# The down projections in pair-groups of 1024 columns with seven block products, and a new order in the first gate-up group

## The chip, the cores and the metric

The kernel runs on one core of one Trainium2 chip, in one launch. The metric is the device time of that launch in microseconds (us); lower is better. The time before is 2096.84 us, the median of three runs (2096.63 to 2097.2 us).

## The reference

Two transformer layers follow each other on one sequence of 256 tokens with a model width of 2048, all in float32. The first layer (four kinds of attention) and the mixers of the second one are not touched by the change. What matters here is the end of the second layer:

```python
y = _rms(h, norm_ffn_g[i])
h = h + (jax.nn.silu(y @ w_gate[i]) * (y @ w_up[i])) @ w_down[i]
y = _rms(h, norm_ple_g[i])
h = h + jax.nn.sigmoid(y @ w_ple_gate[i]) * (p[i] @ w_ple_proj[i])
return _rms(h, final_norm_g)
```

`w_gate` and `w_up` are 2048 x 5632, `w_down` is 5632 x 2048, `w_ple_gate` is 2048 x 2048 and `w_ple_proj` is 256 x 2048.

## The kernel before

**Exact products from halves.** TensorE multiplies in its fast float32 form only what fits a shortened mantissa, so every operand is held as a high part and a remainder, and each product is three matmuls (`three`, L563): high times high, high times low, low times high. ScalarE makes the high part of a weight tile (`hi`, L1068), VectorE the remainder (`lo`, L1497, which overwrites the raw tile). The weights come from memory once; SyncE issues their loads in order of use.

**Units and rings.** The work is a list of 370 units, made by `plan` (L77). A unit is one weight tile of 128 x 2048 values (four blocks of 128 x 512) and, in the units of interest, 24 matmuls of 512 columns. The raw and `lo` tiles share a ring of 5 places and the `hi` tiles one of 4. Between the first and the last unit of the gate-up stage, and nowhere else, the rings have 7 and 5 places (`R_FFN`, `H_FFN`, and `extended`, L359). `Places.take` gives a unit the place that was used longest ago, and the load waits until the unit that used it last is done on TensorE (L490).

**Order of the work.** Every engine runs a fixed program, a loop over the units. In round u, VectorE does, in this order (L2070 to L2086): `side(u)`, small jobs tied to that round; the first two of three weight sums of a later unit; `hide`; the splits of later units (`split_at`, L380: of unit u + 2 where that belongs to a pair group, of u + 3 for the others); the third weight sum; `cross`; and at a group's last unit `finals` or `post`. ScalarE's loop is alike (L1425). An engine can't go past a waiting step, so a late step holds all that is behind it.

**Gate-up groups.** The 11 groups ("ff", j), units 218 to 337 with the down groups between them, are of kind "pair": one takes 512 columns of the gate and 512 of the up matrix, in eight units of two rows of blocks each. `pair_unit` (L659) makes eight block products of a unit, or, in the three units of a group in `SUMMED`, seven (21 matmuls in place of 24), by a scheme of the Strassen kind. The price of the eighth product is: three sums of weight blocks on VectorE (`weight_sums`, L1512 to L1523, issued in round u - 3), a second tile of `hi` and `lo`, sums of token blocks (XS, made once by `token_sums`), and per group a combination of the crossed sums: P1 is copied to E by ScalarE (`begin_sums`), then four additions (`cross`, L1539). `finals` adds the two halves of psA to E (L1551 left, L1553 right). TensorE's products P2 and P3 write the left half of psA, P4 and P8 the right half, P1, P6, P5 and P7 the four quarters of psB. The next group's first P2 waits for the left final of the group before, its P4 for the right one (`await_product`, L637).

**Hidden values.** `gate_tanh` and `hide` turn E into 512 hidden columns of THF. They are transposed by TensorE in round first + 6 of the next group (`TURNH`, L423) and split there into YH (ScalarE) and YL (`low`, VectorE, L1569).

**Down groups.** Before, there are 12 groups of kind "N", each with 512 columns: 4 units of 24 matmuls after gate-up group 3 and again after group 7, 3 units at the end. Their result is added to X in one instruction (L2046). The last four are followed by the squares of X for the norm, and by transposes of X with `turn_h` (`TURN3`), which the last matrix needs.

**Into the gate-up stage.** The groups ("out2", f), units 202 to 217, end in X updates (L2039 in `post`), each followed by squares (ScalarE), and X is transposed in rounds 208, 212, 216 and 219 (`TURN2`). In round 218 VectorE works out the norm's scales. The first gate-up group takes its eight pairs in the order (1, 3, 0, 5, 2, 6, 4, 7), so that its units with seven products are 220, 222 and 224.

Of the kernel before, what the change touches and what calls it, by code (L numbers as in the profile page):

```python
# [24 lines left out]
UNIT = 2048  # L25

# [29 lines left out]
class Group:  # L56


    def __init__(self, number, name, kind, W, cols, parts, first, seven=()):
# [3 lines left out]
        self.area = number % 2  # L63
# [10 lines left out]
FIRST_ORDER = (1, 3, 0, 5, 2, 6, 4, 7)  # L74


def plan(A):  # L77
# [37 lines left out]
    def down(js, turn, areas):  # L115
        for f in range(4):
            group(("down", 4 * turn + f), "N", A["w_down_2"][0], 512 * f,
                  [[(4 * j + k, 4 * (j % 4) + k) for k in range(4)] for j in js], area=areas[f])

    for j in range(11):  # L120
        order = range(8) if j else FIRST_ORDER
        group(("ff", j), "pair", (A["w_gate_2"][0], A["w_up_2"][0]), 512 * j, [PAIRS[q] for q in order],
              [i for i, q in enumerate(order) if q in SUMMED])
        if j in (4, 8):
            down(range(j - 4, j), j // 4 - 1, (3, 2, 0, 1))
# [6 lines left out]
    freed, crossed = {True: 0, False: 0}, 0  # L132
    for g in groups:
        if g.kind != "pair":
# [20 lines left out]
def build_hybrid(nc, A, C, out, scratch):  # L155
    with ExitStack() as ctx:
# [72 lines left out]
        with ExitStack() as p3:  # L229
# [13 lines left out]
            BS = sb("BS", [128, 512], F32, p3)  # L243
        with ExitStack() as p4:
            XS = sb("XS", [128, 3, 2, 512], F32R, p4)
# [4 lines left out]
            for i in range(R, R_FFN):  # L250
                with ExitStack() as here:
                    raw.append(sb(f"raw{i}", [128, UNIT], F32, here))
                lo.append(sb(f"lo{i}", [128, UNIT], F32R, p4))
        with ExitStack() as p4:
# [4 lines left out]
        XF, SF = E[:, 0, :], E[:, 1, :]  # L259
        with ExitStack() as p5:  # L260
# [77 lines left out]
        xf_made, xs_summed, xs_high, xs_low, weights_summed = [sem(n) for n in (  # L338
            "xf_made", "xs_summed", "xs_high", "xs_low", "weights_summed")]
        e0_made, crossed_over, left_done, finals_made, hb_made = [sem(n) for n in (  # L340
            "e0_made", "crossed_over", "left_done", "finals_made", "hb_made")]
# [80 lines left out]
        TURN3 = {347 + 3 * f: f for f in range(4)}  # L422
        TURNH = {named[("ff", j + 1)].first + 6: j for j in range(10)}  # L423
        TURNH[named[("down", 8)].first] = 10
        HALF = [0] * 10 + [1]
        CROSS = {max(named[("ff", j)].seven): j for j in range(11)}
        TANH = {named[("ff", j)].last + 1: j for j in range(11)}
        HIDE = {named[("ff", j)].last + (4 if j < 10 else 3): j for j in range(11)}
# [44 lines left out]
        def sync_program(e):  # L473
# [10 lines left out]
            for u, (g, i) in enumerate(units):  # L484
# [6 lines left out]
                if g.kind == "pair":  # L491
                    gate, up = [w.rearrange("(k p) n -> p k n", p=128)[:, k0:k0 + 2, g.cols:g.cols + 512] for w in g.W]
                    first, second = ((1, 1), (0, 3)) if u in g.seven else ((0, 1), (2, 1))
                    e.dma_start(two(raw[slot][:, :], *first), gate).then_inc(raw_landed[slot], 16)
                    e.dma_start(two(raw[slot][:, :], *second), up).then_inc(raw_landed[slot], 16)
# [19 lines left out]
        def gpsimd_program(e):  # L515
# [39 lines left out]
            e.wait_ge(unit_done, done(("down", 7)))  # L555
            e.dma_start(PP[:, :, :], A["p_2"][0, 0].rearrange("(t p) c -> p t c", p=128)).then_inc(p_landed, 16)

            e.wait_ge(unit_done, done(("down", 11)))
# [3 lines left out]
        def tensor_program(e):  # L562
# [14 lines left out]
            def await_operand(g, i):  # L577
# [15 lines left out]
                elif name == "down":  # L593
                    e.wait_ge(flip_low, HIDDEN + 4 * (n // 4) + i + 1)
# [20 lines left out]
            def await_bank(g):  # L615
                name, n = g.name
                if name == "down" and n < 8:
                    j, f = 4 * (n // 4) + 4, n % 4
                    if f == 0:
                        e.wait_ge(crossed_over, j + 1)  # L620
                    elif f == 1:
                        e.wait_ge(flip_low, HIDDEN + j)
                    else:
                        e.wait_ge(finals_made, 2 * j + f - 1)
                elif name == "proj":
# [4 lines left out]
                    else:  # L630
                        e.wait_ge(finals_made, 22 + n - 3)
                elif name == "down" and n < 10:
                    bank_freed(("proj", n - 6))
# [3 lines left out]
            def await_product(g, product):  # L637

                j = g.name[1]
                if j == 0:  # L640
# [5 lines left out]
                elif j in (5, 9):  # L646
                    first = j - 5
                    if product in ("P1", "P5", "P2", "P4"):
                        bank_freed(("down", first + {"P1": 1, "P5": 0, "P2": 2, "P4": 3}[product]))
                elif product == "P1":  # L650
                    e.wait_ge(crossed_over, j)
                    if j > 1:
                        e.wait_ge(flip_low, HIDDEN + j - 1)
                elif product == "P2":
                    e.wait_ge(finals_made, 2 * j - 1)
                elif product == "P4":
                    e.wait_ge(finals_made, 2 * j)

            def pair_unit(u):  # L659
                g, i = units[u]  # L660
                j = g.name[1]
# [5 lines left out]
                def tokens(k, t):  # L667
                    return [(XH[:, k, t], XL[:, k, t])]

                def product(name, terms):  # L670
                    first = u == begun.get(name)
                    if first:
                        await_product(g, name)
                    for n, (a, b) in enumerate(terms):
                        x = three(BANKS[name], a, b, first and n == 0, u == ended[name] and n == len(terms) - 1)
# [14 lines left out]
                if u in g.seven:  # L690
                    n = (0, 2, 4).index(k0 // 2)
# [1490 lines left out]
```

## Time and profile before

| | |
|---|---|
| median of three runs | 2096.84 us |
| the profiled execution | 2096.8 us |
| its span, first to last instruction | 2094.9 us |
| TensorE busy | 2078.9 us (99%) |
| VectorE busy | 1402.4 us (67%) |
| ScalarE busy | 956.5 us (46%) |
| granted TensorE clock, mean | 0.999 of 2.4 GHz |
| memory read | 394.62 MB, 189 GB/s over the span |
| the chain that ended last | PE 91%, DVE 6%, ACT 1%, issue 1%, DMA 1% |

The profiled execution's 2096.8 us are its span of 2094.9 us and 1.9 us around it. In the profile PE is TensorE, PEld its weight loads, DVE VectorE, ACT ScalarE, SP SyncE. A matmul's row says 0.39 us while the next one starts 0.23 us later: they overlap, so starts are compared, not lengths. Idle time in brackets is that of the engine just before the instruction, with who ended it.

### The profile page before, as it was taken

Reading aid. Unit: us, or ns where it says so; the run is one execution under the profiler, and the core shown is the slowest. Engines: PE = TensorE matmul, PEld = TensorE weight load, DVE = VectorE, ACT = ScalarE, POOL = GpSimd, SP = SyncE. Lnnn points to the kernel's source line nnn. Section 1 sums busy time; section 2 is a strip of 40 time slices with the busy share of each in tenths; the row PEclk is TensorE's granted clock in tenths of the full one; section 3 lists DMA queues with packets and bytes.
Section 4 is the critical chain, followed back from the end, with each engine's and each line's share of the span. In section 5 each row is a group of like instructions: output and inputs, shape, how many; then the busy total and the mean of one; then the engine's idle time right before and its main releaser. Section 6 shows DMA issues by size and latency. Waiting matters only on the chain.

```text
span 2094.9 us, 25122 instructions
## 1 busy us (share of the span) xinstructions
PE 2078.9 (99%) x10496; PEld 1768.9 (84%) x10496; DVE 1402.4 (67%) x1427; ACT 956.5 (46%) x914; POOL 21.1 (1%) x40
## 2 busy tenths in 40 slices
PE   9999999999999999999999999999999999999998
PEld 8888888888888888888999988788888888888887
DVE  5576555665544455455789858999658986587565
ACT  5544443544343434444444455555435544355443
POOL 2000000000000000000000000000000000000000
PEclk9999999999999999999999999999999999999999
DMA  8655455454555555575655564556645566455553
GB/s 248 217 177 180 162 168 193 161 181 169 193 189 193 196 187 198 183 253 189 203 185 164 178 220 161 186 200 219 220 152 199 199 217 218 149 205 188 187 202 120
DMA packets 226144, 398.38 MB, mean 190 GB/s; under 512 B 12610, under 2 KB 57914, under 8 KB 225776
## 3 DMA queue, kind: packets, MB, share of 16 engines
q1 hardware_dynamic: 222752, 387.64, 54.7%
q0 software_dynamic: 2528, 8.00, 1.3%
q8 instruction: 84, 1.38, 0.3%
q10 hardware_dynamic: 752, 1.12, 0.1%
q14 instruction: 28, 0.23, 0.0%
HBM read 394.62 MB, written 2.12 MB: 189 GB/s over the span
## 4 chain that ended last, share of the span: by engine, by line
PE 91%; DVE 6%; ACT 1%; issue 1%; DMA 1%; ACTq 0%; SPq 0%; DVEq 0%
PE psA L564 23%; PE psA L566 23%; PE psA L565 23%; PE psA L737 6%; PE psA L741 3%; PE psB L564 3%; PE psB L565 3%; PE psB L566 3%; DVE lo L1497 2%; DVE CA L1765 1%; PE psB L794 1%; ACT hi L1068 0%; DVE raw L1521 0%; ACT hi L1072 0%; DMA X<-in_x_dram 0%
## 5 line engine op out<-in xcount | busy, mean ns | idle before, releaser
L1497 DVE TENSOR_TENSOR lo<-raw,hi 128x2048 fp32r<-128x2048 f32 (+3 forms) x401 | 889.1, 2228 | 400.7 <-ACT hi L1068 394.9
L1068 ACT ACTIVATE hi<-raw 128x2048 fp32r<-128x2048 f32 (+3 forms) x368 | 679.6, 1859 | 485.9 <-PE psA L566 355.2
L564 PE MATMUL psA<-hi,XHL 128*128 128x512 f32 (+1 forms) x1434 | 560.9, 391 | 1.6 <-DVE E L1551 1.6
L566 PE MATMUL psA<-hi,XHL 128*128 128x512 f32 (+1 forms) x1434 | 556.8, 388 | 0.0
L565 PE MATMUL psA<-lo,XHL 128*128 128x512 f32 (+1 forms) x1434 | 556.4, 388 | 0.0
L564 PEld LDWEIGHTS psA<-hi,XHL 128*128 128x128 f32 x1434 | 269.4, 188 | 56.8 <-DVE E L1551 2.0
L566 PEld LDWEIGHTS psA<-hi,XHL 128*128 128x128 f32 x1434 | 269.2, 188 | 55.8
L565 PEld LDWEIGHTS psA<-lo,XHL 128*128 128x128 f32 x1434 | 269.5, 188 | 53.9
L564 PE MATMUL psA<-hi,YH 128*128 128x512 f32 x488 | 190.6, 391 | 0.0
L566 PE MATMUL psA<-hi,YL 128*128 128x512 f32 x488 | 189.9, 389 | 0.0
L565 PE MATMUL psA<-lo,YH 128*128 128x512 f32 x488 | 189.9, 389 | 0.0
L564 PE MATMUL psA<-XHL,hi 128*128 128x256 f32 (+1 forms) x528 | 150.4, 285 | 0.5 <-DVE lo L1601 0.5
L565 PE MATMUL psA<-XHL,hi 128*128 128x256 f32 (+1 forms) x528 | 149.5, 283 | 0.0
L566 PE MATMUL psA<-XHL,lo 128*128 128x256 f32 (+1 forms) x528 | 149.4, 283 | 0.0
L737 PE MATMUL psA<-XHL,hi 128*128 128x512 f32 x576 | 138.6, 393 | 0.0
L737 PEld LDWEIGHTS psA<-XHL,hi 128*128 128x128 f32 x576 | 106.0, 188 | 21.5 <-issue 0.6
L566 PEld LDWEIGHTS psA<-hi,YL 128*128 128x128 f32 x488 | 91.6, 188 | 19.1
L564 PEld LDWEIGHTS psA<-hi,YH 128*128 128x128 f32 x488 | 91.6, 188 | 18.7
L565 PEld LDWEIGHTS psA<-lo,YH 128*128 128x128 f32 x488 | 91.6, 188 | 18.7
L1072 ACT ACTIVATE hi<-raw 128x2048 fp32r<-128x2048 f32 x33 | 63.2, 1916 | 93.8 <-DVE raw L1517 83.7
L564 PEld LDWEIGHTS psA<-XHL,hi 128*128 128x128 f32 (+1 forms) x528 | 100.8, 191 | 1.0 <-DVE XHL L1608 0.8
L565 PEld LDWEIGHTS psA<-XHL,hi 128*128 128x128 f32 (+1 forms) x528 | 100.8, 191 | 0.2
(385 smaller groups left out, 2030.0 us busy)
## 6 DMA issues: line engine op xcount, KB each, us to landing
raw<-in_w_in_dram SPq DMA_DIRECT2D x158, 1024.0 KB, 4.9
raw<-in_w_gate_dram SPq DMA_DIRECT2D x88, 512.0 KB, 3.8
raw<-in_w_up_dram SPq DMA_DIRECT2D x88, 512.0 KB, 4.7
raw<-in_w_down_dram SPq DMA_DIRECT2D x44, 1024.0 KB, 5.1
raw<-in_w_out_dram SPq DMA_DIRECT2D x32, 1024.0 KB, 5.1
raw<-in_w_branch_dram SPq DMA_DIRECT2D x16, 1024.0 KB, 5.1
raw<-in_w_ple_gate_dram SPq DMA_DIRECT2D x16, 1024.0 KB, 5.1
raw<-in_w_in_dram SPq DMA_DIRECT2D x16, 512.0 KB, 4.7
```

Of the source, the lines that this page charges most:

```text
L564: e.matmul(dst, A2[0], B2[0], start=first, stop=False, skip_group_check=True)
L565: e.matmul(dst, A2[0], B2[1], start=False, stop=False, skip_group_check=True)
L566: return e.matmul(dst, A2[1], B2[0], start=False, stop=last, skip_group_check=True)
L737: e.matmul(both, hh[:, s], XHL[:, kb, :, :].rearrange("p a t -> p (a t)"), start=i == 0 and n < 2, stop=False, skip_group_check=True)
L741: x = e.matmul(both[:, 256:512], ll[:, s], XH[:, kb, :], start=False, stop=i == len(g.parts) - 1 and n >= 14, skip_group_check=True)
L794: x = e.transpose(ps[:, k, 128 * t:128 * t + 128], src(t, k), ID[:, :])
L1068: e.activation(hi[h_slot[u]][:, m], raw[l_slot[u]][:, m], ACT.Copy).then_inc(hi_made, 1)
L1072: e.activation(hi[th_slot[u]][:, :], raw[t_slot[u]][:, :], ACT.Copy).then_inc(hi_made, 1)
L1497: e.tensor_tensor(lo[l][:, m], raw[l][:, m], hi[h][:, m].bitcast(F32), ALU.subtract).then_inc(lo_made, 1)
L1765: x = e.scalar_tensor_tensor(out=CA[:, c, :], in0=HP[:, c, j:j + 256], scalar=CW[:, 4 * j + c:4 * j + c + 1], in1=CA[:, c, :], op0=ALU.mul ...
```

## The change

The down groups become pair groups of 1024 columns, two for each turn (six in all, with 8, 8, 8, 8, 6 and 6 units; the number of units stays, and the last two groups, 4 and 5, are units 342 to 347 and 348 to 353). The pairs 0 and 2 of each (`HIDDEN_SUMMED`) are made with seven block products. So each has weight sums, a second tile, a `cross` and `finals`, and `add_hidden` adds the crossed sums to X before the finals are added there. The pairs' token sums are now made for the hidden values too (j = 0, 1, 4, 5, 8, 9), in the tiles FORM and FHL, by `copy_block`, `token_sums`, `high_forms` and `low_forms`; the first of the four formed blocks replaces the block of the tokens that isn't used any more. The first gate-up group runs its pairs as (1, 0, 3, 2, 5, 4, 6, 7), with units 219, 221 and 223 as those with seven products, and its first such unit makes its products in another order. `hide` comes a round earlier. The ring sizes and the range in which they are extended stay.

```diff
+USUAL = ("P1", "P6", "P5", "P7", "P2", "P3", "P4")
+LATE = ("P1", "P6", "P2", "P3", "P4", "P5", "P7")
...
-FIRST_ORDER = (1, 3, 0, 5, 2, 6, 4, 7)
+FIRST_ORDER = (1, 0, 3, 2, 5, 4, 6, 7)
+HIDDEN_SUMMED = (0, 2)
+LAST_ORDER = (1, 0, 3, 2, 4, 5)
...
-    def down(js, turn, areas):
-        for f in range(4):
-            group(("down", 4 * turn + f), "N", A["w_down_2"][0], 512 * f,
-                  [[(4 * j + k, 4 * (j % 4) + k) for k in range(4)] for j in js], area=areas[f])
+    w_down = A["w_down_2"][0]
+
+    def down(turn, orders):
+        for q, order in enumerate(orders):
+            group(("down", 2 * turn + q), "pair", (w_down, w_down), (1024 * q, 1024 * q + 512),
+                  [[(16 * turn + 2 * p + k, 2 * p + k) for k in range(2)] for p in order],
+                  [i for i, p in enumerate(order) if p in HIDDEN_SUMMED])
...
-    down((8, 9, 10), 2, (0, 1, 0, 1))
+    down(2, (LAST_ORDER, range(6)))
...
-        TURN3 = {347 + 3 * f: f for f in range(4)}
+        TURN3 = {352: 0, 353: 1, 355: 2, 356: 3}
...
-        HIDE = {named[("ff", j)].last + (4 if j < 10 else 3): j for j in range(11)}
+        HIDE = {named[("ff", j)].last + (2 if j == 10 else 3): j for j in range(11)}
+        SQUARE4 = {352: 0, 353: 1}
...
+                elif name == "ple" and n < 2:
+                    e.wait_ge(finals_made, 2 * named[("down", 5)].pair + n + 1)
...
                     elif product == "P1":
                         e.wait_ge(ss3_made, 4)
+                    elif product == "P5":
                         e.wait_ge(flip_low, SECOND + 4)
...
+            def copy_block(key, turned, half, scale):
+
+                count, slot = FORMS[key]
+                e.wait_ge(flip_turned, turned + 1)
+                if count >= 5:
+                    e.wait_ge(unit_done, named[("down", 2 * ((count - 3) // 2) - 1)].last + 1)
+                e.activation(FORM[slot][:, 0, 0:256], c4(psB[:, half, :])[:, 0, :], ACT.Copy, scale=scale).then_inc(forms_copied, 1)
+
+            def high_forms(key, turned, dst):
+                count, slot = FORMS[key]
+                e.wait_ge(forms_summed, count + 1)
+                e.wait_ge(flip_low, turned + 1)
+                e.activation(dst, FORM[slot][:, 0, 256:384], ACT.Copy).then_inc(forms_high, 1)
+                e.wait_ge(forms_low, 2 * count + 1)
+                e.activation(FHL[slot][:, 0, :], FORM[slot][:, 1, :], ACT.Copy).then_inc(forms_high, 1)
...
+            def token_sums(key, turned, half, scale):
...
+                e.wait_ge(flip_high, turned + 1)
+                e.wait_ge(forms_copied, count + 1)
+                finish(e.scalar_tensor_tensor(out=s1, in0=a22, scalar=scale, in1=a21, op0=ALU.mult, op1=ALU.add))
                 e.tensor_tensor(s3, a11, a21, ALU.subtract)
-                finish(e.tensor_tensor(s1, a21, a22, ALU.add))
                 finish(e.tensor_tensor(s2_, s1, a11, ALU.subtract))
...
+            def low_forms(key, dst, dstH):
+                count, slot = FORMS[key]
+                e.wait_ge(forms_high, 2 * count + 1)
+                e.tensor_tensor(dst, FORM[slot][:, 0, 256:384], dstH.bitcast(F32), ALU.subtract).then_inc(forms_low, 1)
+                e.wait_ge(forms_high, 2 * count + 2)
+                e.tensor_tensor(FHL[slot][:, 1, :], FORM[slot][:, 1, :], FHL[slot][:, 0, :].bitcast(F32),
+                                ALU.subtract).then_inc(forms_low, 1)
...
+            def add_hidden(g):
+
+                c = slice(g.cols[0], g.cols[0] + 1024)
+                e.wait_ge(crossed_over, g.pair + 1)
+                e.tensor_tensor(X[:, 0, c], X[:, 0, c], flat(E[:, 0:2, :]), ALU.add)
+                e.tensor_tensor(X[:, 1, c], X[:, 1, c], flat(E[:, 2:4, :]), ALU.add).then_inc(e_read, 1)
...
+                if u - 1 in TURNH and ("hidden", TURNH[u - 1]) in FORMS:
+                    k = 4 * (TURNH[u - 1] % 4)
+                    low_forms(("hidden", TURNH[u - 1]), YL[:, k, 128:256], YH[:, k, 128:256])
...
+                    if ("hidden", j) in FORMS:
+                        token_sums(("hidden", j), HIDDEN + j, 0, 1.0)
                     low(HIDDEN + j, YL[:, js, :], YH[:, js, :], HALF[j], 1.0)
```

ScalarE calls `copy_block` and `high_forms` in the rounds in which VectorE calls `token_sums` and `low_forms`, ahead of its splits of that round. The places that the rings give by the new plan, where the prediction speaks of them: unit 348 is loaded into the place of unit 344, unit 347 into another one that unit 344 frees, and both loads are issued when unit 344 is done.

## Rows read from the trace of the kernel before

**Rows 1.** The page: busy time of TensorE.
```profile
PE 2078.9 (99%) x10496; PEld 1768.9 (84%) x10496; DVE 1402.4 (67%) x1427; ACT 956.5 (46%) x914; POOL 21.1 (1%) x40
```

**Rows 2.** Waits of TensorE from 1050 us on: us in total, times, longest.
```profile
PE psA L564 <- DVE E L1551: 1.6, 1, 1.6
PE psB L794 <- DVE THF L1560: 1.1, 1, 1.1
PE psB L564 <- DVE XHL L1573: 0.4, 1, 0.4
```

**Rows 3.** Timeline of TensorE: first matmuls of units 258 and 274.
```profile
1486.42 0.39 PE L564 MATMUL psB<-hi,YH 128*128 128x512 f32 x1
...
1573.46 0.39 PE L564 MATMUL psB<-hi,XHL 128*128 128x512 f32 x1
```

**Rows 4.** Timeline of VectorE, gate-up group 1, crossing to left final.
```profile
1342.85 0.69 DVE L1542 TENSOR_TENSOR E<-E,psB 128x512 f32<-128x512 f32 x1 [2.53 <-ACT E L1322]
...
1345.50 1.22 DVE L1521 TENSOR_TENSOR raw<-raw 128x1024 f32<-128x1024 f32 x1
...
1347.36 2.28 DVE L1497 TENSOR_TENSOR lo<-raw,hi 128x2048 fp32r<-128x2048 f32 x1
1349.56 0.69 DVE L1517 TENSOR_TENSOR raw<-raw 128x512 f32<-128x512 f32 x1
1350.16 1.22 DVE L1569 SCALAR_TENSOR_TENSOR YL<-psB,YH 128x1024 fp32r<-128x1024 f32 x1
1351.29 3.95 DVE L1497 TENSOR_TENSOR lo<-raw,hi 128x1536 fp32r<-128x1536 f32 x2
...
1359.83 1.22 DVE L1551 TENSOR_TENSOR E<-E,psA 128x1024 f32<-128x1024 f32 x1
```

**Rows 5.** Timeline of TensorE: the first P2 of gate-up group 2.
```profile
1361.95 0.39 PE L564 MATMUL psA<-hi,XHL 128*128 128x512 f32 x1
```

**Rows 6.** Timeline of ScalarE: the split of unit 235, then of 236.
```profile
1352.64 3.28 ACT L1068 ACTIVATE hi<-raw 128x2048 fp32r<-128x2048 f32 x2
```

**Rows 7.** Timeline of VectorE, rounds 216 to 219.
```profile
1262.04 0.29 DVE L1530 TENSOR_TENSOR E<-E 128x128 f32<-128x128 f32 x1 [5.58 <-ACT E L1081]
1262.24 0.28 DVE L1531 TENSOR_TENSOR E<-E 128x128 f32<-128x128 f32 x1
1262.56 0.29 DVE L1532 TENSOR_TENSOR E<-E 128x128 f32<-128x128 f32 x1
...
1263.50 1.66 DVE L1573 SCALAR_TENSOR_TENSOR XHL<-psB,VC,XHL 128x256 fp32r<-128x256 f32 x4 [0.32 <-ACT XHL L1106]
...
1272.79 1.40 DVE L2039 SCALAR_TENSOR_TENSOR X<-X,SM,psA 128x512 f32<-128x512 f32 x2
1275.73 0.16 DVE L1494 TENSOR_REDUCE SM<-SM 128x2 f32<-128x8 f32 x1 [1.54 <-ACT psB L1114]
...
1278.59 3.96 DVE L1497 TENSOR_TENSOR lo<-raw,hi 128x1536 fp32r<-128x1536 f32 x2
```

**Rows 8.** Timeline of TensorE: the first P4 of unit 218.
```profile
1274.58 0.39 PE L564 MATMUL psA<-hi,XHL 128*128 128x512 f32 x1
```

**Rows 9.** Timeline of TensorE: the eight transposes of a side job, and what follows.
```profile
1474.62 1.04 PE L794 MATMUL psB<-ID,THF 128*128 128x128 f32 x8
1475.41 0.47 PE L564 MATMUL psA<-hi,XHL 128*128 128x512 f32 x1
```

**Rows 10.** Timeline of SyncE: two pair units loaded together.
```profile
1342.21 0.37 SPq L494 DMA_DIRECT2D raw<-in_w_gate_dram  x1
...
1343.65 0.47 SPq L495 DMA_DIRECT2D raw<-in_w_up_dram  x1
```

**Rows 11.** One line's instructions: the second load of a pair unit (L495).
```profile
DMA to landing us min/median/max: 4.4/4.7/8.6
```

**Rows 12.** Stretches: us, busy of PE, PEld, DVE, ACT, POOL, PEclk, DMA share, GB/s.
```profile
2085.00:2090.00 5.00, 0.22 (x2) 0.02 (x1) 3.23 (x13) 1.92 (x6) 0.00 (x0) 0.93 0.24 87
2090.00:2094.90 4.90, 0.00 (x0) 0.00 (x0) 0.53 (x2) 0.71 (x2) 0.00 (x0) 0.50 0.58 214
```

More of the change, by code:

```diff
@@ L243, in build_hybrid, with form_tile @@
             BS = sb("BS", [128, 512], F32, p3)
+        FORM, FHL = [], []
+        def form_tile(where, n):
+            for i in range(len(FORM), len(FORM) + n):
+                with ExitStack() as here:
+                    FORM.append(sb(f"FORM{i}", [128, 2, 384], F32, here))
+                FHL.append(sb(f"FHL{i}", [128, 2, 384], F32R, where))
         with ExitStack() as p4:
-            XS = sb("XS", [128, 3, 2, 512], F32R, p4)
+            form_tile(p4, 4)
             THF = sb("THF", [128, 1024], F32, p4)
@@ L491, in sync_program @@
                 if g.kind == "pair":
-                    gate, up = [w.rearrange("(k p) n -> p k n", p=128)[:, k0:k0 + 2, g.cols:g.cols + 512] for w in g.W]
+                    left, right = [w.rearrange("(k p) n -> p k n", p=128)[:, k0:k0 + 2, c:c + 512] for w, c in zip(g.W, g.cols)]
                     first, second = ((1, 1), (0, 3)) if u in g.seven else ((0, 1), (2, 1))
-                    e.dma_start(two(raw[slot][:, :], *first), gate).then_inc(raw_landed[slot], 16)
-                    e.dma_start(two(raw[slot][:, :], *second), up).then_inc(raw_landed[slot], 16)
+                    e.dma_start(two(raw[slot][:, :], *first), left).then_inc(raw_landed[slot], 16)
+                    e.dma_start(two(raw[slot][:, :], *second), right).then_inc(raw_landed[slot], 16)
                     continue
@@ L616, in await_bank @@
                 name, n = g.name
[L617 to L625, printed above, removed]
+                if name == "proj":
                     if n == 0:
@@ L630, in await_bank @@
                     else:
[L631 to L633 removed]
+                        e.wait_ge(finals_made, 2 * named[("ff", 10)].pair + n - 1)
+                elif name == "ple" and n < 2:
+                    e.wait_ge(finals_made, 2 * named[("down", 5)].pair + n + 1)
                 elif g.number >= 2:
@@ L667, in tokens, with product @@
                 def tokens(k, t):
-                    return [(XH[:, k, t], XL[:, k, t])]
-                def product(name, terms):
-                    first = u == begun.get(name)
+                    return AH[:, k, t], AL[:, k, t]
+                def product(p, terms):
+                    first = u == begun[p]
                     if first:
-                        await_product(g, name)
-                    for n, (a, b) in enumerate(terms):
-                        x = three(BANKS[name], a, b, first and n == 0, u == ended[name] and n == len(terms) - 1)
+                        await_product(g, p)
+                    for m, (a, b) in enumerate(terms):
+                        x = three(BANKS[p], a, b, first and m == 0, u == ended[p] and m == len(terms) - 1)
                     return x
@@ L1392, in post @@
                     squares(n, X, ss3, ss3_made)
-                elif name == "down" and n >= 8:
-                    e.wait_ge(bank_dve, g.freed)
-                    squares(n - 8, X, ss4, ss4_made)
+                elif g.name == ("down", 5):
+                    e.wait_ge(finals_made, 2 * g.pair + 2)
+                    squares(2, X, ss4, ss4_made)
+                    squares(3, X, ss4, ss4_made)
                 elif name == "proj":
@@ L1948, in side @@
                 if u - 1 in TURN2 and TURN2[u - 1] < 3:
-                    token_low(TURN2[u - 1])
+                    f = TURN2[u - 1]
+                    low_forms(("x", f), XL[:, 4 * f, 128:256], XH[:, 4 * f, 128:256])
+                if u - 1 in TURNH and ("hidden", TURNH[u - 1]) in FORMS:
+                    k = 4 * (TURNH[u - 1] % 4)
+                    low_forms(("hidden", TURNH[u - 1]), YL[:, k, 128:256], YH[:, k, 128:256])
                 if u == named[("ff", 10)].last:
```

182 lines of the change are left out of this document (93 added, 89 removed).

## The prediction

> **What bounds the kernel now.** I read the page first: TensorE is busy 99% of the span [rows 1]. So the time is the number of matmuls times their distance, plus the few waits. Next its waits: from the last mixer groups to the end there are three of note, 1.6, 1.1 and 0.4 us [rows 2]. A wait is counted from the modelled end of the matmul before it, 0.16 us behind the place of the next start, so they cost about 1.8, 1.3 and 0.6. They are the first P2 of gate-up group 1, the transposes in round 342, and the P1 of unit 220. Then the distance: units 258 to 273 are 384 matmuls in 1573.46 - 1486.42 = 87.04 us, 0.2267 us each [rows 3]: 5.44 us a unit, 4.76 with seven products. Last the question on which the change hangs: how late may VectorE be? From crossing to left final in gate-up group 1 its row of work has no hole; the final ends at 1361.05 [rows 4] and TensorE's first P2 starts at 1361.95 [rows 5]. With 0.04 for the wake the room is **0.86 us**. What is put between those two beyond that is waited for in each group. The 67% of VectorE's busy time hides this.
>
> **Matmuls removed.** Six down groups with two such units each: 12 x 3 x 0.2267 = **-8.2 us**, all on the path.
>
> **New work in five gate-up groups.** Starts in rows 4 give: two weight sums 1.86, a split 2.20, the third sum 0.60, `low` 1.13, a double split 3.86 (3.95 less overlap), the four crossings 2.65, a final 1.22. In groups 1, 2, 5, 6 and 9 the hidden values with token sums (j = 0, 1, 4, 5, 8) are turned in round first + 6, right in this row of work; j = 9 falls into group 10, where `proj` covers it (its P2 comes two units later). `token_sums` is four 128-wide instructions; a step is 0.20 without and 0.32 with a wait between [rows 7]: 1.1 in all. `low_forms` is a 128-wide one (0.29), then a wait for ScalarE's 384-wide copy, which itself waits for that one (0.6, by the widths around it), then a 384-wide one (0.5): 1.4. ScalarE's split of unit 235 [rows 6] moves behind this from 1352.64 to 1357.1 and ends at 1359.0; VectorE comes to it at 1359.5, so it costs nothing more. So 2.5 - 0.86 = 1.6 us, five times: **+8.1**. Ends: 1.1 each if those waits vanish (2.0 of pure work), 2.2 if the moved split comes 0.6 late. The wait isn't handed on: `cross` starts on TensorE's last P7, and VectorE has idled 2.53 us before it [rows 4]. After groups 4 and 8 no forms are made and the chain is as today, so the first down group waits for nothing. From one down group to the next VectorE has five units for one crossing and two X additions; a final there waits only for its matmuls.
>
> The Trainium skill ("VectorE: DVE Perf Modes", section "The DRAIN you can't avoid") says that a semaphore between two such instructions costs nothing extra. The rows differ by 0.12 us, so the measurement stands; by the page the five groups would be 1.2 us cheaper.
>
> **The front.** With unit 219 as the first one with seven products, round 216 also has its first sums, and round 217 its double split, all ahead of the X update of out2 group 3. Today that starts at 1272.79 and ends at 1274.19 [rows 7]; the P4 of unit 218 needs it at 1274.58 [rows 8]. New: `token_sums` waits for the high parts (about 1263.15), 1.1; `low` 1.66 -> 1265.9; sums 1.86, split of 218 2.20, third sum 0.60 -> 1270.5; `low_forms` 1.4 -> 1271.9; the split of 219 waits for ScalarE, whose copy was held by `low_forms` (0.9), then 3.86 and 0.1 more wait -> 1276.8; X update 1.40 -> 1278.2. P4 waits **3.7** (1.9 without the waits between the two engines).
> Then P5 of unit 219, which now waits for the last token block: squares 1.54, scales 1275.73 to 1278.59 = 2.86 [rows 7], sums of unit 221 1.86, split of 220 2.20 and 0.60, `low` 1.66: 10.7 us after the X update. TensorE has 12 matmuls, transposes (0.8) [rows 9] and 15 matmuls, 6.9 us. P5 waits **3.8**. Both are followed by a new order that does help: the crossing comes a unit earlier, the left final half a us ahead of P2, so today's 1.8 goes, and so does the 0.6. Front: 3.7 + 3.8 - 1.8 - 0.6 = **+5.1**, lower end +3.3, upper +6.
>
> **The end.** Here the rings are short (5 and 4) and a unit with seven takes two places. In round 342 `hide` comes earlier and frees the transposes, but the sums of unit 343 wait for its load ahead of the split of 342, and ScalarE's copy of `proj` 3, which P4 needs, stands behind the second split of 343: 0.4 and 0.8, about the 1.3 of today: 0. Then unit 348. Its load can be issued when 344 is done, as third and fourth of four: 1.4 us behind the first [rows 10], landing 4.4 to 8.6 [rows 11]; I take 6.6, between median and longest since two units share the queue: 8.2 us after the end of 344 with 0.2 for the issue. VectorE waits there in round 345, ahead of the split of 347. From the landing to the left final of down group 4: sums 1.86, split 2.20, 0.60, crossing 2.65, double split 3.86, X additions 2.26, sums of 350 1.86, split 2.20, 0.60, final 1.22 = 19.3. So P2 of unit 348 starts 27.5 us after the end of 344; TensorE alone needs 4.76 + 5.44 + 5.44 + 2.72 = 18.4. **+9.2**, in three pieces: 2.3 before 347, 1.5 before 348, 5.4 at its P2. Ends 7.0 and 11.2 by the landing.
> The first `ple` unit now waits for the last left final. From the end of 348 VectorE has ScalarE's split 1.9, seven splits 15.4, crossing 2.65, additions 2.26, two `low` 3.3, final 1.2 = 26.8, and 4.3 of waiting for loads (351 goes into 348's place, 5 us to land), 31.1; TensorE 5.44 + 4.76 + 5.44 + 2 x 6.24 = 28.1: **+3.0** (0 to 4). The later squares and `low` of X end before unit 357 asks.
>
> **Sum.** -8.2 + 8.1 + 5.1 + 9.2 + 3.0 = +17.2 on the profiled execution's 2096.8 (the median is 2096.84, the same): **2114.0 us**. All low ends give 2104, all high ends 2121.
>
> **Rivals.** *VectorE takes it up (other side).* Place: between crossing and final. It idles 2.5 us before each crossing, and much more in the down groups; if it worked ahead there, all new waits and today's three would go: 2096.8 - 8.2 - 1.8 - 0.6 - 1.3 = 2084.9. It decides from where the new waits together stay below 7.7 us (11.9 - 4.2). For it: the 67%. Against: the loop's order; what is added stands behind the crossing and the landing, where the row has no hole. 0.10.
> *The end keeps up.* If unit 348's load and the last final come in time, +5.1 + 8.1 - 8.2 = +5.0: 2101.8. For it: today the splits are far ahead there; against: the place isn't free earlier. 0.12.
> *The clock falls in a wait.* After the last matmul the granted clock was full in most of the stretch to 2090 (0.93 in the mean) and 0.50, the 1.2 GHz level, in the next [rows 12]; TensorE had done nothing for some 4 us. The 5.4 us wait at unit 348 could do the same. At half the clock the nine matmuls left of that unit cost 2 us more, a whole unit 5.4; taking 3.5: 2117.5. For it: the wait's length; against: 1.6 us did nothing, and 3.8 may be too short too. 0.20. The Trainium skill ("TensorE: Matmul & The Clock Gate", section "HAM oscillation — how this bites in real kernels") speaks of just this: idle gaps between bursts of matmuls bring the clock back to its lower level, and the next burst starts slow.
>
> **Chances.** Forecast 0.55 (2104 to 2119), the clock 0.20, the end keeps up 0.12, VectorE takes it up 0.10, some mix near today's time 0.03. Within 0.2% (4.2 us, about what a measurement of this kernel can tell from no change) lies the mix and a little of the second rival's: 0.05. Faster 0.10, slower 0.85. The range, 2101 to 2120, takes in the second and third rival; the first is left out with the thin ends.
>
> **What would show it.** In the waits of the changed kernel: five of about 1.6 us on L1551's successor in the gate-up groups 2, 3, 6, 7 and 10; one of 3.7 before the P4 of unit 218 on the X update, one near 3.8 in unit 219 on `low`; at the end one on a split, one on a final of over 5 us, and one before the first `ple` unit. In VectorE's timeline: six short instructions more between crossing and final, and a hole ended by a load near the end. I'm wrong if VectorE idles as long as today before the finals, or if the holes at the end fall together with no wait of TensorE.

## The result, and the profile after

The changed kernel takes **2116.84 us** (median of four runs, 2116.22 to 2118.41), against 2096.88 for the kernel before (median of four, beside it): 1.0097 times as long, 95% interval 1.0085 to 1.0109. That is 20 us slower. The profiled execution has a span of 2114.9 us, 20.0 more than before, and all that follows is read from it. One correction of what stands before: the down groups of the first two turns follow gate-up groups 4 and 8, as the prediction has it, and not 3 and 7, as the section on the kernel says. TensorE's granted clock is 0.996 in the mean, 0.999 before.

Busy time first, to be laid beside [rows 1]:

```profile
PE 2079.8 (98%) x10460; PEld 1765.0 (83%) x10460; DVE 1487.6 (70%) x1550; ACT 980.8 (46%) x950; POOL 21.1 (1%) x40
```

VectorE works 85 us more, and its share is still only 70%. The loss can't be seen here: 36 matmuls fewer are recorded (as many as the change removes), yet the span grew. It is in TensorE's waits, the view of [rows 2], again from 1050 us on (us in total, times, longest):

```profile
PE psA L589 <- DVE E L1601: 6.8, 5, 1.4
PE psA L589 <- DVE X L1601: 6.6, 2, 5.1
PE psA L589 <- DVE X L2094: 3.5, 1, 3.5
PE psB L813 <- DVE XHL L1623: 1.6, 1, 1.6
PE psA L589 <- DVE lo L1528: 1.4, 2, 0.8
PE psB L589 <- DVE lo L1528: 1.4, 1, 1.4
PE psB L589 <- DVE XHL L1623: 0.7, 1, 0.7
PE psA L589 <- ACT PJ L1425: 0.5, 1, 0.5
```

Three waits of 3.1 us in all have become fourteen of 22.5 us (one of 0.2 us near the end is left out on both sides). The first line is the left final of five gate-up groups, the second the left finals of the last two down groups (5.05 and 1.54), the third the P4 of unit 218. The first matmul of one of the five, with its two predecessors, in TensorE's timeline (as [rows 5]):

```profile
1366.66 0.39 PE L590 MATMUL psB<-lo,FHL 128*128 128x512 f32 x1
1366.88 0.39 PE L591 MATMUL psB<-hi,FHL 128*128 128x512 f32 x1
1368.65 0.50 PE L589 MATMUL psA<-hi,XHL 128*128 128x512 f32 x1 [1.38 <-DVE E L1601]
```

It starts 1.77 us after its predecessor, where 0.23 is usual, so a wait that reads 1.38 costs 1.54. The unit as a whole takes 1.67 us longer, as the second start after a wait comes late too, 0.34 us after the first. VectorE's row of work that it waits for, as in [rows 4]:

```profile
1348.01 0.69 DVE L1581 TENSOR_TENSOR E<-E,psB 128x512 f32<-128x512 f32 x1 [3.12 <-ACT E L1348]
...
1355.32 0.28 DVE L1564 SCALAR_TENSOR_TENSOR FORM<-psB,FORM 128x128 f32<-128x128 f32 x1
1355.63 0.29 DVE L1565 TENSOR_TENSOR FORM<-FORM 128x128 f32<-128x128 f32 x1
1355.84 0.28 DVE L1566 TENSOR_TENSOR FORM<-FORM 128x128 f32<-128x128 f32 x1
1356.16 0.29 DVE L1567 SCALAR_TENSOR_TENSOR FORM<-psB,FORM 128x128 f32<-128x128 f32 x1
...
1361.37 0.28 DVE L1573 TENSOR_TENSOR YL<-FORM,YH 128x128 fp32r<-128x128 f32 x1
1362.24 0.56 DVE L1575 TENSOR_TENSOR FHL<-FORM,FHL 128x384 fp32r<-128x384 f32 x1 [0.59 <-ACT FHL L1108]
...
1367.39 1.21 DVE L1601 TENSOR_TENSOR E<-E,psA 128x1024 f32<-128x1024 f32 x1
```

From the crossing's first instruction to the start of the left final it is 19.38 us, 16.98 before: 2.40 more, of which 1.05 are the four token sums and 1.35 the two `low` instructions with the 0.59 of waiting for ScalarE between them. VectorE still stands idle for 3.12 us right ahead of the crossing.

Where the 20.0 us arise, from the first matmuls of the units (the twelve units with three matmuls fewer go from 5.44 to 4.76 each):

| | forecast | measured |
|---|---|---|
| 12 units with seven products | -8.2 | -8.2 |
| five gate-up groups | +8.1 | +8.3 |
| front, units 218 to 226 | +5.1 | +5.0 |
| unit 342 | 0 | +0.3 |
| end: up to the P2 of unit 348 | +9.2 | +8.1 |
| end: lower clock behind it | 0 (a rival) | +2.6 |
| end: ahead of the `ple` units | +3.0 | +3.8 |
| elsewhere | 0 | +0.2 |
| sum | +17.2 | +20.1 |

### The profile page after: what moved, and what is told of

It reads as the page before. It is cut to its first block, busy times and chain, and to the rows that moved or that the text cites. A ratio compares the mean times of both kernels' runs of the same rounds, so it can differ in the third digit from the quotient of the medians.

```text
span 2114.9 us, 25312 instructions
## 1 busy us (share of the span) xinstructions
PE 2079.8 (98%) x10460; PEld 1765.0 (83%) x10460; DVE 1487.6 (70%) x1550; ACT 980.8 (46%) x950; POOL 21.1 (1%) x40
## 4 chain that ended last, share of the span: by engine, by line
PE 85%; DVE 10%; ACT 2%; issue 2%; DMA 1%; SPq 0%; ACTq 0%; DVEq 0%
PE psA L589 23%; PE psA L591 22%; PE psA L590 22%; PE psA L756 6%; DVE lo L1528 4%; PE psA L760 3%; PE psB L589 2%; PE psB L590 2%; PE psB L591 2%; DVE CA L1815 1%; ACT hi L1088 1%; PE psB L813 1%; DMA raw<-in_w_down_dram 1%; DVE raw L1552 1%; DVE raw L1548 0%
## 5 line engine op out<-in xcount | busy, mean ns | idle before, releaser
L1528 DVE TENSOR_TENSOR lo<-raw,hi 128x2048 fp32r<-128x2048 f32 (+3 forms) x413 | 907.9, 2212 | 372.5 <-ACT hi L1088 365.4
L589 PE MATMUL psA<-hi,XHL 128*128 128x512 f32 (+1 forms) x1434 | 562.6, 392 | 11.9 <-DVE E L1601 6.8
L589 PE MATMUL psA<-hi,YH 128*128 128x512 f32 x544 | 213.7, 393 | 6.9 <-DVE X L1601 5.1
L590 PE MATMUL psA<-lo,YH 128*128 128x512 f32 x544 | 212.4, 390 | 0.0
L591 PE MATMUL psA<-hi,YL 128*128 128x512 f32 x544 | 212.4, 390 | 0.0
L1092 ACT ACTIVATE hi<-raw 128x2048 fp32r<-128x2048 f32 x45 | 86.3, 1917 | 135.3 <-DVE raw L1548 105.2
L589 PEld LDWEIGHTS psA<-hi,YH 128*128 128x128 f32 x544 | 102.6, 189 | 29.9 <-DVE X L1601 5.5
L591 PEld LDWEIGHTS psA<-hi,YL 128*128 128x128 f32 x544 | 102.5, 188 | 21.6
L590 PEld LDWEIGHTS psA<-lo,YH 128*128 128x128 f32 x544 | 102.6, 189 | 20.9
```

Of the source, the lines that this page charges most:

```text
L589: e.matmul(dst, A2[0], B2[0], start=first, stop=False, skip_group_check=True)
L590: e.matmul(dst, A2[0], B2[1], start=False, stop=False, skip_group_check=True)
L591: return e.matmul(dst, A2[1], B2[0], start=False, stop=last, skip_group_check=True)
L1092: e.activation(hi[th_slot[u]][:, :], raw[t_slot[u]][:, :], ACT.Copy).then_inc(hi_made, 1)
L1528: e.tensor_tensor(lo[l][:, m], raw[l][:, m], hi[h][:, m].bitcast(F32), ALU.subtract).then_inc(lo_made, 1)
```

## The experiments

Each single run is set against the changed kernel's 2116.84 us, and read by its trace. Beside these runs the kernel before took 2096.11 to 2096.78 us. A single run moves by a us without a cause that I could name: the wait at the first matmul of unit 342 is 0.62 us in the changed kernel, and 0.78, 1.30 and 1.65 us in three runs whose edit comes behind it. So parts are compared where whole times can't decide. Line numbers of a kernel are its own.

**The front's new order, undone.**

```diff
-FIRST_ORDER = (1, 0, 3, 2, 5, 4, 6, 7)
+FIRST_ORDER = (1, 3, 0, 5, 2, 6, 4, 7)
...
-                    elif product == "P5":
...
-                    late = u == fives[0] and g.name in (("ff", 0), ("down", 4))
+                    late = u == fives[0] and g.name == ("down", 4)
```

> The changed kernel with the old order of the first gate-up group (1, 3, 0, 5, 2, 6, 4, 7) and its old waits. My theory: the new order costs 5.0 us net, since it puts a double split ahead of the last X update; with the old one the 3.5 us wait before the P4 of unit 218 and the first low stretch of the granted clock go, the waits of 1.6 and 0.4 us of the kernel before come back, and the time is about 2111.8. Rival (the new order helps, and the loss has its cause in the longer work on token forms): the time is 2117 or more.

2112.57 us. Units 218 to 226 now cost 1.3 us more than in the kernel before, not 5.0. The P4 of unit 218 waits 0.81 us in place of 3.53 (the token sums of the mixers' values still stand in round 216), 226's wait of 1.6 is back, and the clock stays full at the front. The five waits and the end are as in the changed kernel. So 3.7 us of the front's 5.0 are the new order. The other 1.3 I put down to the token sums, which stand there in both kernels; no run here takes them away alone.

**`high_forms` and `low_forms` a round later.**

```diff
-                if u - 1 in TURNH and ("hidden", TURNH[u - 1]) in FORMS:
+                if u - 2 in TURNH and ("hidden", TURNH[u - 2]) in FORMS:
...
```

> The changed kernel with high_forms and low_forms of the hidden values one round later, behind the group's finals; token_sums stays where it is. My theory: low_forms with its wait (1.4 us) leaves the row between crossing and left final, the five waits fall from 1.38 us to near 0.2 (1.1 of sums less 0.86 of room), and the time from 2116.8 to about 2111. Rival (the five waits come from VectorE having more to do in all, not from where it stands): the waits stay at 1.3 to 1.4 us and the time at 2116 to 2117.

2114.34 us. The waits of TensorE have no line for E any more, and a longer one for `lo`, by six:

```profile
PE psB L589 <- DVE lo L1528: 3.8, 6, 1.2
```

Five of the six are 0.52 to 0.53 us long and new, each four units after the P2 that no longer waits (units 238, 246, 286, 294, 334), and ahead of it a split that comes late. So the five waits did hang on that row; but what is taken out of it makes a later step late. The five P2 units lose 1.35 each and the five later ones gain 0.85: 2.5 of the 8.3 us come back, where I had expected some 6.

**The token sums of the hidden values made twice.**

```diff
-                finish(e.scalar_tensor_tensor(out=s1, in0=a22, scalar=scale, in1=a21, op0=ALU.mult, op1=ALU.add))
...
+                for m in range(2 if key[0] == "hidden" else 1):
+                    finish(e.scalar_tensor_tensor(out=s1, in0=a22, scalar=scale, in1=a21, op0=ALU.mult, op1=ALU.add))
...
```

> The changed kernel, with the four 128-wide sums of the hidden values' tokens made twice in each of the six groups that have them (same values, so the output is the same). They cost 1.1 us in VectorE's row between the crossing and the left final. My theory: each us put there is waited for one to one at the next group's first P2, as the 1.38 us waits have no slack behind them: the five waits grow from 1.38 to about 2.5 us, nothing else moves, and the time is 5 x 1.1 = 5.5 above the 2116.8 of the changed kernel: about 2122.5 us. Rival (the waits come from ScalarE's copies or from the load, and VectorE's row has room): less than 2 us more.

2125.02 us. The five waits are 2.52 to 2.57 us:

```profile
PE psA L589 <- DVE E L1604: 12.7, 5, 2.6
```

That is 5.9 us more in all, for 5.5 expected. The doubled sums add 1.17 us to the row (1354.74 to 1356.96 in place of 1355.32 to 1356.37) and each wait grows by as much: one to one. The other 2.3 us weren't expected. Just behind one of these five waits the granted clock fell (at 1370.3 us, for 3.41 us): unit 234 took 0.9 us longer than the other four, and unit 235 took 0.7 more than usual. Most of the rest is unit 342 (+0.8), whose split was late.

**The last turn as before.** The last down groups are again four of kind "N" of three units each (called `end` here), without seven products:

```diff
-    down(2, (LAST_ORDER, range(6)))
+    for f in range(4):
+        group(("end", f), "N", w_down, 512 * f,
+              [[(4 * j + k, 4 * (j % 4) + k) for k in range(4)] for j in (8, 9, 10)], area=f % 2)
...
```

> The changed kernel with the last turn of down projections as before: four groups of 512 columns, three units of 24 matmuls each, the old squares and transposes. My theory: the end costs 12 us (four units with seven products save 2.7, the waits and the low clock cost 14.7), so the time is about 2104.8, with no low stretch of the clock after 1990. Rival (the end's loss is what the loss of the groups before hands on): the time is 2110 or more.

2103.01 us: 13.8 less. 11.9 of it arise from unit 341 on, with four units at 5.44 again. The other 1.7 I hadn't counted: without seven products in the last turn the forms for j = 8 aren't made, and the fifth P2 wait (unit 330) goes too. The seven products of the last turn cost 13.8 us and are the largest part of the loss.

**Which step of the end.** Two edits at unit 348. The first has VectorE split unit 347 ahead of the sums of unit 348, in round 345:

```diff
-                if u in sums_at:
+                if u in sums_at and u != 345:
...
+                if u == 345:
+                    weight_sums(sums_at[u], False)
```

> The changed kernel, with one pair of steps exchanged: in round 345 VectorE splits unit 347 first and makes the sums of unit 348 (which wait for its late load) after that. My theory: the P2 of unit 348 waits for VectorE's row, which begins at the landing of unit 348; with the split of 347 done in the time in which VectorE waits for it, that row ends 1 to 2 us sooner, so the wait of 5.05 us becomes 3 to 4 us; the clock falls all the same, and the time is 1 to 2 us less: about 2115.5 us. Rival (the load alone decides, or the split of 347 was in nobody's way): no change in the wait.

2116.53 us. The wait at the P2 is 5.05 us as before the edit, and yet the rival is wrong as well. VectorE's left final, counted from its split of unit 346, comes 20.85 us later in place of 21.81: 0.96 us earlier. But TensorE too reached unit 348 earlier, since its wait ahead of it fell from 1.38 to 0.53. Both ends of the wait moved. The gain of 0.9 us was then covered by unit 342, which took 0.7 more in this run. The size was at the lower edge of what I had expected (1 to 2 us), its place wasn't where I had put it.

The second makes unit 348 with eight products (its products of the second half of the tokens read a block that a formed one has replaced, so those rows of columns 1024 to 2047 of the last down projection are not the reference's):

```diff
-                  [i for i, p in enumerate(order) if p in HIDDEN_SUMMED])
+                  [i for i, p in enumerate(order) if p in HIDDEN_SUMMED and (turn, q, p) != (2, 1, 0)])
```

> The changed kernel, with one unit less with seven products: the pair 0 of the last down group (unit 348) is made with eight products; unit 350 stays. It puts 3 matmuls (0.68 us) back and takes away the two places that unit 348 held, its double split and its sums. My theory: the row of work from the crossing to the left final of down group 4 gets shorter by the sums and one split, so the 5.05 us wait before the first P2 after it goes down to 4 us or less although that P2 is now the first matmul of the unit; the time is 2 to 4 us less, about 2113.5 us; if the clock stays full, 2 us less again. Rival (the end's loss hangs on unit 350 or on the first ple unit, not on 348): 0.7 us more, 2117.5.

2115.88 us, 1.0 less. From the first matmul of unit 347 to the end it is 2.8 us less, inside the 2 to 4 us that I expected; 1.6 more at the front and 1.0 more at unit 342, both ahead of the edit, hide most of it. The P2, now the first matmul of the unit, waits 4.40 us, where I had expected 4 or less. So unit 348 is one reason of the end's loss and not all of it: the row between crossing and left final is that long in any case.

**The clock, with the waits filled.** In the changed kernel TensorE's granted clock was 0.5, the 1.2 GHz level, for 6.83 us from 1277.5 us on and again for 6.83 us from 1977.3 us on. Before, no such stretch lay ahead of the last matmul. Here are the stretch of the second fall and the one after it (us, busy of PE, PEld, DVE, ACT, POOL, PEclk, DMA share, GB/s), and then the first matmuls in the fall:

```profile
1977.00:1984.00 7.00, 5.08 (x12) 4.02 (x13) 4.67 (x5) 0.77 (x1) 0.00 (x0) 0.52 0.00 0
1984.00:1991.00 7.00, 7.00 (x32) 5.75 (x32) 2.29 (x1) 2.63 (x2) 0.00 (x0) 0.99 0.93 294
```

```profile
1978.92 0.80 PE L589 MATMUL psA<-hi,YH 128*128 128x512 f32 x1 [5.05 <-DVE X L1601]
1979.52 0.63 PE L590 MATMUL psA<-lo,YH 128*128 128x512 f32 x1
1979.94 0.63 PE L591 MATMUL psA<-hi,YL 128*128 128x512 f32 x1
1980.37 0.63 PE L589 MATMUL psA<-hi,FHL 128*128 128x512 f32 x1
```

At this level the matmuls stand 0.43 us apart in place of 0.23. To read the price, both waits were filled with matmuls whose result isn't used. First the front:

```diff
+                        if u == named[("ff", 0)].first and p == "P4":
+                            for _ in range(15):
+                                e.matmul(BANKS["P6"], tokens(k0, T0)[0], block(0)[0], start=True, stop=True, skip_group_check=True)
```

> The changed kernel with 15 matmuls more that nobody reads, made in unit 218 while TensorE waits for the X update. My theory: the granted clock stays full there; the matmuls of units 218 and 219 then take 2.9 us less, and P5 of unit 219 waits that much longer, near 3.6 us in place of 0.67, since both wait for the same work of VectorE. Time within 0.5 us of 2116.8. Rival (the low clock in that stretch costs on the path): 2.9 us less, 2113.9.

2117.15 us. The clock stays full, and the P5 of unit 219 now waits 3.35 us in place of 0.67: the time is the same. At the front the lower clock was free, because the next wait was for the same row of VectorE. Then the end:

```diff
                     for m in LATE if late else USUAL:
                         x = product(m, [seven[m]])
+                        if u == 348 and m == "P7":
+                            for _ in range(7):
+                                x = product(m, [seven[m]])
```

> The changed kernel, with 21 more matmuls in unit 348 ahead of its P2: its P7 is begun anew seven times, which leaves the result as it is and keeps TensorE busy for 21 x 0.2267 = 4.8 of the 5.05 us in which it waits there. My theory: the wait before the P2 shrinks to about 0.3 us and costs nothing of its own, since VectorE's final decides the P2's start; the granted clock now stays full, and the second half of unit 348 and unit 349 lose the 2.6 us that I read as the price of the lower clock: the waits after it (transposes of unit 353 and P2 of unit 354, VectorE's row) grow by part of it, so the time is 0 to 2.6 us less, and I take 1.5: 2115.3 us. Rival (the clock's price is real and VectorE has room after it): the whole 2.6, 2114.2. Rival (the slow stretch hid under the next waits, as at the front): no change, 2116.8.

2117.25 us, 0.4 more, though the part in question went as expected. The wait is short and the clock full:

```profile
1979.01 0.39 PE L590 MATMUL psB<-lo,FHL 128*128 128x512 f32 x1
1979.23 0.39 PE L591 MATMUL psB<-hi,FHL 128*128 128x512 f32 x1
1979.90 0.50 PE L589 MATMUL psA<-hi,YH 128*128 128x512 f32 x1 [0.28 <-DVE X L1604]
```

From the end of unit 342 to the last matmul it is 1.55 us less: 2.4 gained in units 348 and 349, and 0.8 of that given back at unit 351, whose split is now late. The whole time hides it: units 218 to 226 took 1.6 more in this run (below), and 1.1 came after the last matmul, where ScalarE's issue of two output transfers took 2.03 us, 0.96 in the changed kernel, and the activation behind it began late.

**A combination.** If the loss was placement, then the middle's eight units can be had alone. Both turns in the middle keep seven products, the last turn and `FIRST_ORDER` are as before, and the hidden values' sums are made six rounds after the transposes, with their splits right behind, in VectorE's idle time ahead of the next crossing. ScalarE copies both blocks out in the old round, so the sums now read them there and not in psB:

```diff
-                if u - 1 in TURNH and ("hidden", TURNH[u - 1]) in FORMS:
-                    k = 4 * (TURNH[u - 1] % 4)
+                if u - 6 in TURNH and ("hidden", TURNH[u - 6]) in FORMS:
+                    k = 4 * (TURNH[u - 6] % 4)
+                    hidden_sums(("hidden", TURNH[u - 6]))
...
-                    if ("hidden", j) in FORMS:
-                        token_sums(("hidden", j), HIDDEN + j, 0, 1.0)
```

> A combination: the two turns of down groups in the middle as in the changed kernel (eight units with seven products), the last turn and the first gate-up group as in the kernel before, and the sums and splits of the hidden values' tokens six rounds later than the transposes, in the time in which VectorE stands idle ahead of the next crossing (ScalarE only copies both blocks out in the old place). My theory says that the loss was all placement: eight units at -0.68 are -5.4, the five waits go, the front costs 1.3 (0.8 and 0.6 for the token sums of the mixers' values in rounds 216 and 217, which I left where the change has them): about 2092.7 us, 4 us below the kernel before. Rival (the added 128- and 384-wide instructions are on the path wherever they stand): the waits come up elsewhere, and the time is 2097 or more.

**2093.06 us** (11 runs, 2092.66 to 2093.62) against 2096.78 of the kernel before: 0.9983 times, interval 0.9974 to 0.9992. Eight units at -0.68 are -5.4; 1.3 is lost at the front as expected and 0.9 in two small P2 waits (units 250 and 298). VectorE's timeline ahead of the crossing of gate-up group 2 shows where the work went:

```profile
1380.23 0.28 DVE L1580 TENSOR_TENSOR FORM<-FORM 128x128 f32<-128x128 f32 x1
...
1382.62 0.56 DVE L1590 TENSOR_TENSOR FHL<-FORM,FHL 128x384 fp32r<-128x384 f32 x1 [0.59 <-ACT FHL L1114]
1384.43 2.29 DVE L1533 TENSOR_TENSOR lo<-raw,hi 128x2048 fp32r<-128x2048 f32 x1 [1.25 <-ACT hi L1091]
1386.64 0.68 DVE L1596 TENSOR_TENSOR E<-E,psB 128x512 f32<-128x512 f32 x1
```

No P2 wait of over 1 us is left but the one that the kernel before has too. But the moved work does not quite fit the idle time. The 1.25 us behind it are not to spare: the split waits there for ScalarE's copy, and the crossing follows the split with no idle time between. In the kernel before, the crossing begins 0.63 us after ScalarE begins to copy P1 (1342.22 and 1342.85). In groups 2 and 3 of this kernel that copy, and the crossing of group 3, are at:

```profile
1385.23 0.60 ACT L1354 ACTIVATE E<-psB 128x512 f32<-128x512 f32 x1 [0.83 <-PE psA L593]
```

```profile
1427.65 0.60 ACT L1354 ACTIVATE E<-psB 128x512 f32<-128x512 f32 x1 [0.42 <-PE psA L593]
```

```profile
1429.48 0.68 DVE L1596 TENSOR_TENSOR E<-E,psB 128x512 f32<-128x512 f32 x1
```

So the crossing is 0.78 us late in group 2 and 1.20 in group 3. The room of 0.86 covers the first. Of the second 0.34 is left over: that is the wait at unit 250 (it reads 0.17, with the 0.16 that such a reading lacks). Groups 6 and 7 are alike, with the wait at unit 298.

**The combination with three more steps moved**: the norm's scales from round 218 to 226, the mixers' `high_forms` and `low_forms` a round later, `hide` of group 10 a round earlier.

```diff
-                if u == 218:
+                if u == 226:
...
-                if u - 1 in TURN2 and TURN2[u - 1] < 3:
+                if u - 2 in TURN2 and TURN2[u - 2] < 3:
```

> The combination before it (2093.1 us), with three more steps moved: the norm's scales for X from round 218 to round 226 (the row that the X update and the split of unit 220 stand in), the sums' splits of the mixers' token blocks one round later than their sums, and the hidden values of gate-up group 10 a round earlier. My theory: the waits of 0.8, 0.6 and 1.6 us at the front and the one of 1.0 before the transposes of unit 342, each counted 0.16 to 0.2 longer, go: about 2088.5 us. Rival (what is moved makes the next thing in its row late): 2091 or more.

**2091.48 us** (11 runs, 2091.27 to 2092.18) against 2096.56: 0.9976 times, interval 0.9967 to 0.9985, so 5 us faster than the kernel before and the best here. It fell 3 us short of what I expected, where the rival had put it. Its waits:

```profile
PE psA L591 <- DVE E L1616: 2.0, 3, 1.6
PE psB L591 <- DVE lo L1533: 0.6, 1, 0.6
```

The waits of 0.8 and 1.0 us went, and the one of 0.6 is 0.14. The first P2 of group 1 still waits 1.6. I had put that down to the scales of round 218; VectorE's timeline says otherwise:

```profile
1307.70 2.29 DVE L1533 TENSOR_TENSOR lo<-raw,hi 128x2048 fp32r<-128x2048 f32 x1 [0.19 <-ACT hi L1095]
1309.91 0.68 DVE L1596 TENSOR_TENSOR E<-E,psB 128x512 f32<-128x512 f32 x1
...
1317.21 1.22 DVE L1616 TENSOR_TENSOR E<-E,psA 128x1024 f32<-128x1024 f32 x1
```

A split stands right ahead of the crossing, with no idle time, because the last unit with seven products (224) comes so late in this group's order. And the scales, now in round 226, stand ahead of a split there (1319.48 to 1322.33 us): the splits behind it are late, unit 230 waits 0.63 us, and unit 228 comes 0.4 late. Moved work was free only where there was a hole.

## Why the prediction was right, and where its sum was off

The forecast was 2114.0 us in a range of 2101 to 2120, slower with 0.85; it is 2116.84.

**The matmuls removed**: -0.68 us in each of twelve units, as worked out.

**The five gate-up groups**: right by the mechanism and the size. Measured 2.40 us of added work less the 0.86 of room, forecast 2.5 less 0.86. The doubled sums show that nothing else has slack there. What the Trainium skill says ("VectorE: DVE Perf Modes", section "The DRAIN you can't avoid") of a semaphore between two such instructions, that it costs nothing extra, does not hold here either: the four token sums start 0.31, 0.21, 0.32 and 0.21 us apart, the longer steps being those with a wait between.

**The front**: the sum of 5.1 is what was measured (5.0), but not in the way I said. The P4's wait was 3.53 for 3.7. Of the 3.8 us wait forecast at the P5 only 0.67 came; in place of the rest the matmuls ran at the lower clock. The filled wait shows the two to be the same time.

**The end** is where the sum failed, at +14.5 for +12.2, in three steps.
- *The places.* "Its load can be issued when 344 is done, as third and fourth of four" is wrong, and the last sentence of the section on the change is wrong about unit 347. It is units 346 and 347 that go into places freed together, by unit 343; unit 348 is loaded alone after 344 (end 1952.46):

```profile
1948.14 0.47 SPq L519 DMA_DIRECT2D raw<-in_w_down_dram  x1
1948.65 0.54 SPq L520 DMA_DIRECT2D raw<-in_w_down_dram  x1
1952.66 0.37 SPq L519 DMA_DIRECT2D raw<-in_w_down_dram  x1
1953.07 0.47 SPq L520 DMA_DIRECT2D raw<-in_w_down_dram  x1
```

  Its two halves landed 5.43 and 6.45 us after their issue, the second at 1959.52, 7.1 us after the end of 344 and not 8.2. From there my row held: VectorE begins at once and the P2 starts 19.4 us later, forecast 19.3.

```profile
1959.54 1.23 DVE L1552 TENSOR_TENSOR raw<-raw 128x1024 f32<-128x1024 f32 x1 [1.41 <-DMA raw<-in_w_down_dram]
...
1977.65 1.21 DVE L1601 TENSOR_TENSOR X<-X,psA 128x1024 f32<-128x1024 f32 x1
```

  So +8.1 and not +9.2, with 5.05 us of it at the P2 itself, forecast 5.4, and 1.38 ahead of unit 348, forecast 1.5. The 2.3 forecast ahead of unit 347 didn't come; TensorE waited 0.80 ahead of unit 346, for its split.
- *The clock.* It fell in that wait, the rival to which I gave 0.20, and cost 2.6 us: 2.0 in the nine matmuls left of unit 348 (forecast 2), 0.6 in unit 349. The filled wait gave 2.4 back. It was no alternative to the forecast but came on top of it, and a wait of over 5 us in the forecast should have carried it with a higher chance: in all six runs with this wait of 5.0 to 5.1 us the clock fell, in five of them within the wait and in one 0.3 us behind it. What the Trainium skill says ("TensorE: Matmul & The Clock Gate", section "HAM oscillation — how this bites in real kernels") agrees: the burst after a gap starts slow.
- *Ahead of the `ple` units*: two waits (1.56 at transposes of X, 1.54 at a left final), each with its 0.2, and 0.25 at unit 351: 3.8 for 3.0.

The first step made the end 1.1 us too dear, the other two 3.4 too cheap. That these partly cancel is luck.

**The other rivals.** VectorE did not take the work up, though it idles just ahead of each crossing: a fixed order fills no hole by itself. The combination shows that it does so when the steps are put there by hand. The end did not keep up. Run with the last turn as before, the kernel takes 2103.0 us. That this is near the 2101.8 of that rival says nothing for it: the rival had twelve cheaper units and five waits, this run has eight and four.

## What to carry to other kernels

Count added work against the slack of the row in which it stands, from the instruction that starts the row to the one that TensorE waits for: here 0.86 us of room decided the matter, under a busy share of 67%. Work made for later can go ahead of the event that starts the row, where the engine stands idle; in four groups it cost 6.7 us behind the crossing and 0.9 before it, and even that only where it outgrew the idle time by more than the room. And look at what is still left to run before a saving is taken at the end of a stage with short rings: the last four units saved 2.7 us and cost 13.8 more than they gave.

## What was not expected of the hardware

The same wait does not always bring the clock down. Seven kernels have the front's wait of 3.5 us unfilled, each looked at once. In the changed kernel and three others the granted clock was 0.5 for 6.83 us from within the wait (1276.9 to 1277.8 us); in the run with doubled sums for 3.41 us; in the one with unit 348 made of eight products for 3.41 us from 1279.3 on and again for 3.41 us from 1289.5 on; in the one with the end's wait filled not at all there, and for 3.41 us from 1289.5 on. The last two cost 1.6 us more at the front than the others, since their stretch from 1289.5 us on came behind the P5's wait, where no other wait hid it. That wait was 3.39 us long in one of them and 1.81 in the other. In the run with the front's wait filled the P5 waited 3.35 us, and in the one with doubled sums 1.82, and no fall followed. Of five waits of 2.5 us one was followed by a fall, of those of 1.7 us and below none. A slow stretch costs only what the next wait for the same row doesn't cover: nothing at the front of the changed kernel, 1.6 us in those two, 2.6 us at the end.
